# Last two projection units done slice by slice, with the first DeltaNet block prepared between the slices

## The reference

```python
h = rms_norm(x, g_mix)
proj = h @ w_in                       # q, k, v, z, b, a of DeltaNet; q, k, v and indexer of the sparse attention
y_a = gated_deltanet(...)             # chunks of 64 tokens, 4 heads:
#   gamma = exp(decay_i - decay_j) below the diagonal
#   A = strict_lower((k*beta) @ k.T * gamma);  T = inv(I + A)
#   u = T @ v*beta;  w = T @ k*beta*exp(decay);  qk = q @ k.T * gamma
#   scan over the 16 chunks:  v_new = u - w S;  o = q S + qk v_new;  S = S*last + k_dec.T v_new
y_b = indexed_sparse_attention(...)   # keep the 256 best keys of each query, softmax over these
x += concat(y_a, y_b) @ w_out;  x += cross_attention(...);  x += swiglu(...)
```

## Time and profile before

| what | us |
|---|---|
| median of 3 runs | 1855.81 |
| lowest, highest | 1853.48, 1856.25 |
| the profiled execution, its own time | 1854.56 |
| its span, first to last instruction | 1852.8 |
| PE busy | 1758.6 (95%) |
| DVE, ACT, POOL busy | 828.9, 675.0, 708.6 |
| mean granted TensorE clock | 0.974 of full |

### The profile page before, as it was taken

The page is one execution under the profiler, slowest core; times in us unless marked ns, Lnnn a source line. Parts: engine busy times, 40 slices in busy tenths (PEclk is TensorE's granted clock), DMA queues, the critical chain, the costliest instruction groups (busy, mean ns, idle before and its releaser), DMA issues.

```text
span 1852.8 us, 26846 instructions
## 1 busy us (share of the span) xinstructions
PE 1758.6 (95%) x10357; PEld 1410.4 (76%) x10357; DVE 828.9 (45%) x1436; ACT 675.0 (36%) x1414; POOL 708.6 (38%) x436
## 2 busy tenths in 40 slices
PE   6999999999987879799999999999999999999999
PEld 5888878877765665466877777888888888888887
DVE  4289878611115886565664365321331331233133
ACT  5366587688841223566035633010010001001000
POOL 4322234333232442464343225334424443343431
PEclk9999999999995999799999999999999999999999
DMA  7130111222230021002111011111111111111112
GB/s 235 55 83 24 35 35 46 69 91 80 80 126 1 2 93 50 21 2 92 62 31 46 24 35 34 50 54 46 45 45 57 45 45 57 45 45 45 57 34 91
DMA packets 112028, 102.33 MB, mean 55 GB/s; under 512 B 5132, under 2 KB 99391, under 8 KB 111679
## 3 DMA queue, kind: packets, MB, share of 16 engines
q1 hardware_dynamic: 109630, 92.67, 16.4%
q10 hardware_dynamic: 2304, 8.39, 1.1%
HBM read 87.42 MB, written 13.63 MB: 55 GB/s over the span
## 4 chain that ended last, share of the span: by engine, by line
PE 86%; DVE 7%; ACT 2%; issue 2%; SPq 1%; POOL 1%; DMA 0%; DVEq 0%; ACTq 0%
PE ps L1393 9%; PE ps L1395 9%; PE ps L1394 9%; PE ps L409 7%; PE ps L437 7%; PE ps L439 7%; PE ps L438 7%; PE ps L410 6%; PE ps L411 6%; PE ps L975 2%; PE ps L1224 2%; PE ps L1070 2%; PE ps L1249 2%; PE ps L1235 2%; PE ps L927 1%
## 5 line engine op out<-in xcount | busy, mean ns | idle before, releaser
L749 POOL TENSOR_TENSOR WS<-WR,zero 128x1024 fp32r<-128x1024 f32 (+1 forms) x119 | 228.2, 1918 | 883.5 <-PE ps L411 303.6
L751 POOL TENSOR_TENSOR WS<-WR,WS 128x1024 fp32r<-128x1024 f32 (+1 forms) x119 | 302.6, 2543 | 9.4
L1393 PE MATMUL ps<-HS,WS 128*128 128x512 f32 x704 | 274.7, 390 | 3.2 <-DVE HS L345 3.2
L1395 PE MATMUL ps<-HS,WS 128*128 128x512 f32 x704 | 274.4, 390 | 0.0
L1394 PE MATMUL ps<-HS,WS 128*128 128x512 f32 x704 | 274.1, 389 | 0.0
L456 DVE TENSOR_TENSOR X<-X,ps 128x512 f32<-128x512 f32 x272 | 183.8, 687 | 156.8 <-PE ps L439 155.3
L409 PE MATMUL ps<-HS,WS 128*128 128x512 f32 (+2 forms) x592 | 227.3, 384 | 3.8 <-ACT raw L1517 3.8
L410 PE MATMUL ps<-HS,WS 128*128 128x512 f32 (+2 forms) x592 | 224.5, 379 | 0.0
L411 PE MATMUL ps<-HS,WS 128*128 128x512 f32 (+2 forms) x592 | 224.2, 379 | 0.0
L2220 DVE TENSOR_TENSOR prod<-sil,ps 128x512 f32<-128x512 f32 x44 | 30.3, 688 | 394.7 <-PE ps L1395 394.7
L1740 ACT ACTIVATE sil<-ps 128x512 f32<-128x512 f32 x44 | 26.3, 598 | 395.0 <-PE ps L1395 395.0
(11 more groups left out here) (302 smaller groups left out, 2939.7 us busy)
## 6 DMA issues: line engine op xcount, KB each, us to landing
WR<-in_w_gu SPq DMA_DIRECT2D x44, 512.0 KB, 3.8
WR<-in_w_in SPq DMA_DIRECT2D x36, 512.0 KB, 3.8
WR<-in_w_down SPq DMA_DIRECT2D x22, 512.0 KB, 3.6
X<-in_x SPq DMA_DIRECT2D x8, 1024.0 KB, 8.4
dsa_spill<-cacc ACTq DMA_DIRECT2D x12, 512.0 KB, 2.6
KW<-in_w_xkv SPq DMA_DIRECT2D x8, 512.0 KB, 4.8
WR<-in_w_out SPq DMA_DIRECT2D x8, 512.0 KB, 3.6
out<-X SPq DMA_DIRECT2D x8, 512.0 KB, 2.6
```

The lines of the kernel that those rows point to most:

```text
L749: pool.tensor_tensor(hi, w, bc(zero1[:, 0:1], [P, cols]), ALU.add).then_inc(w_hi, 1)
L751: pool.tensor_tensor(lo, w, hi.bitcast(F32), ALU.subtract).then_inc(w_split, 1)
L1393: pe.matmul(ps[:, b0 + half, :], lo, HS[:, 0, k, c], start=(k == 0), stop=False)
L1395: mm = pe.matmul(ps[:, b0 + half, :], hi, HS[:, 0, k, c], start=False, stop=(k == KT - 1))
```

## The change

Units 14 and 15 (`LAST2`) leave the unit loop. They are done together by `last_two(k, first)`, one slice of the contraction for both, 12 matmuls a slice, into four banks (4 to 7) that keep accumulating, in the order 6, 5, 4, 3, 2, 1, 0, 7. `gdn_order` gets a step `beside`, which runs before each part of block 0: slices 6 and 5 stand before `diff`, slices 4, 3, 2 behind GQ, halves of slices 1 and 0 before z1, y2, z2, y3, and slice 7 before z3. The meeting and its waits are gone. A semaphore `hs_done` counts slices 6, 5, 4, 3 as done, and those who write over a slice wait for it (POOL at 1 for `gU` and at 4 for X0, DVE at 4 for A). ACT's copies and spills of the two units stand in part "k" of block 0. `PREP` has a new order for all blocks: k behind level 3, v behind level 4. A and Q move from part "k" to part "gq" on DVE, X0 to "gq" and TT0 before X1 on POOL, k and v go through banks 1 and 3, and z5 waits for `vb0`. The split of the second output weight (n = `N_OUT` + 1) moves on POOL behind X5 of block 0. `sd` on ACT moves from v = 13 to v = 12. The masks start later: the thresholds at p = 10 to 14 and not 2 to 8, the first mask at 15 and not 8, and from p = 28 on the table is the old one. SP loads `vraw` after the spills and `rsH`, `kD` behind the k transposes of block 3 and `zS` behind its v transposes.

```diff
+        PREP = (["gq", "x0"] + [f"{x}{s}" for s in (1, 2, 3) for x in "yz"]
+                + ["k", "y4", "z4", "v", "y5", "z5", "w", "next"])
+        LAST2 = (N_Z + 14, N_Z + 15)
...
+            run(beside, "diff")
             prep(-1, "next")
             for part in PREP:
+                run(beside, part)
                 prep(0, part)
...
-            sp.wait_ge(met, 3 * MEET_MIX)
+            d0d.wait(sp, "rs")
...
+            gp.wait(sp, "k1", 3)
+            sp.dma_start(kD[:, :, :], back[1]).then_inc(qk_in[1], 16)
             gp.wait(sp, "v1", 3)
-            sp.dma_start(kD[:, :, :], back[1]).then_inc(qk_in[1], 16)
...
-            for n in range(RING, N_OUT + RING - 1):
+            for n in range(RING, N_OUT + 1):
...
-                    pool.wait_ge(met, 3 * MEET_MIX)
                     g0d.wait(pool, "bk2")
+                    pool.wait_ge(hs_done, 1)
...
-                if part == "k":
+                if part == "gq":
                     gd.wait(pool, "A", b)
+                    if b == 0:
+                        pool.wait_ge(hs_done, 4)
...
+                    if b == 0 and part == "z3":
+                        split_of(N_OUT + 1)
...
-            for v in range(16):
+            for v in range(14):
                 up_pe(pe, N_Z + v, HS, WHOLE)
...
-            meet(0, pe)
+            def last_two(k, first, ready=None):
+                for i in first:
+                    n = LAST2[i]
+                    if k == 6:
+                        pe.wait_ge(w_split, n + 1)
+                    for half, (c, w) in enumerate(WHOLE):
+                        if ready:
+                            ready[i][half]()
+                        acc = ps[:, 4 + 2 * i + half, 0:w]
+                        hi, lo = (WS[:, n % RING, s, k * P:(k + 1) * P] for s in (0, 1))
+                        pe.matmul(acc, lo, HS[:, 0, k, c:c + w], start=(k == 6), stop=False)
+                        pe.matmul(acc, hi, HS[:, 1, k, c:c + w], start=False, stop=False)
+                        mm = pe.matmul(acc, hi, HS[:, 0, k, c:c + w], start=False, stop=(k == 7))
+                    if k == 7:
+                        mm.then_inc(unit_done, 1)
+                    elif i == 1 and k >= 3:
+                        mm.then_inc(hs_done, 1)
+            def beside(part):
+                if part == "diff":
+                    last_two(6, (0, 1), ...)
+                    last_two(5, (0, 1))
+                    pe.wait_ge(up_freed, ups[N_Z + 13] + 1)
+                elif part == "x0":
+                    for k in (4, 3, 2):
+                        last_two(k, (0, 1))
+                elif part == "z1":
+                    last_two(1, (0,))
...
+                elif part == "z3":
+                    last_two(7, (0, 1))
...
+                        if s == 5:
+                            gd.wait(pe, "vb0", b)
...
+            def beside(part):
+                if part == "k":
+                    spill(14)
+                    spill(15)
...
-            MASKS = {8: [(2, "count"), (2, "tie")], 10: [(2, 0), (2, 1)], 12: [(2, "kept"), (2, "out"), (2, "bias")],
+            MASKS = {15: [(2, "count"), (2, "tie")], 16: [(2, 0), (2, 1)], 17: [(2, "kept"), (2, "out")],
...
             def threshold(p):
-                if p == 2:
+                if p == 10:
+                    dve.wait_ge(unit_done, ups[LAST2[1]] + 1)
...
-                if part == "k":
+                if part == "gq":
...
+                    if b == 0:
+                        dve.wait_ge(hs_done, 4)
                     gd.mark(dve.tensor_tensor(Am[:, :], ps[:, 2, :], gam[:, 0, :], ALU.mult), "A", b)
```

More of the change, by code:

```diff
@@ L500, in build_layer @@
         g0d = steps("g0_dve", ["z", "max", "sp", "g", "ek", "rk2", "eq", "bk2", "ned", "ked"])
-        gp = steps("gdn_pe", ["diff", "GQ", "k0", "k1", "v0", "v1"]
-                   + [f"{x}{s}" for s in LV for x in "yz"] + ["w0", "w1"])
-        gd = steps("gdn_dve", ["A", "Q", "nk0", "kd0", "nk1", "kd1", "T0", "vb0", "vb1"]
-                   + [f"{x}{s}" for s in LV for x in (("T", "TT") if s < 5 else ("TT",))])
+        gp = steps("gdn_pe", ["diff", "GQ"] + [f"{x}{s}" for s in (1, 2, 3) for x in "yz"]
+                   + ["k0", "k1", "y4", "z4", "v0", "v1", "y5", "z5", "w0", "w1"])
+        gd = steps("gdn_dve", ["A", "Q", "T0"] + [f"{x}{s}" for s in (1, 2, 3) for x in ("T", "TT")]
+                   + ["nk0", "kd0", "nk1", "kd1", "T4", "TT4", "vb0", "vb1", "TT5"])
+        hs_done = sem("x_slices_done")
         ga = steps("gdn_act", ["gam"] + [f"y{s}" for s in LV] + ["w0", "w1"])
-        gl = steps("gdn_pool", ["gU", "dM", "gD", "X0", "X1", "TT0"] + [f"X{s}" for s in LV if s > 1])
+        gl = steps("gdn_pool", ["gU", "dM", "gD", "X0", "TT0", "X1"] + [f"X{s}" for s in LV if s > 1])
         sp_, sd_ = steps("scan_pe", ["v", "s", "o"]), steps("scan_dve", ["S", "ot"])
@@ L578, in bc @@
             return ap.to_broadcast(shape)
-        PREP = ["gq", "k", "x0", "v"] + [f"{x}{s}" for s in LV for x in "yz"] + ["w", "next"]
+        PREP = (["gq", "x0"] + [f"{x}{s}" for s in (1, 2, 3) for x in "yz"]
+                + ["k", "y4", "z4", "v", "y5", "z5", "w", "next"])
+        LAST2 = (N_Z + 14, N_Z + 15)
         def half_unit(e):
@@ L591, in bc_bank, with gdn_order @@
             return e % 3 if e < 8 else e % 2
-        def gdn_order(prep, tail, new_v=None, from_state=None, to_state=None, out=None):
+        def gdn_order(prep, tail, new_v=None, from_state=None, to_state=None, out=None, beside=None):
             def run(step, c):
@@ L837, in decayed @@
                 last = lastb[:, :].rearrange("p (a k) -> p a k", a=2)[:, :, 2 * (c + 1):2 * (c + 1) + 2]
+                if c == 0:
+                    for s in spilled:
+                        pool.wait_ge(s, 16 * 8)
                 sd_.wait(pool, "S", c)
@@ L1019, in _ @@
                     g0p.mark(mm, "cols")
-            meet(0, pe)
+            def last_two(k, first, ready=None):
[17 more added lines that the diff above has]
+                if part == "diff":
+                    last_two(6, (0, 1), ((lambda: g0a.wait(pe, "rows"), lambda: g0a.wait(pe, "last")),
+                                         (lambda: g0d.wait(pe, "eq"), lambda: d0a.wait(pe, "sd"))))
+                    last_two(5, (0, 1))
[5 more added lines that the diff above has]
+                    last_two(1, (0,))
+                elif part == "y2":
+                    last_two(1, (1,))
+                elif part == "z2":
+                    last_two(0, (0,))
+                elif part == "y3":
+                    last_two(0, (1,))
+                elif part == "z3":
+                    last_two(7, (0, 1))
             def per_unit(b, fn):
@@ L1209, in tail @@
                     o_tr(3 * (h - 5) // 2 + 2)
-            gdn_order(prep, tail, new_v, from_state, to_state, out)
+            gdn_order(prep, tail, new_v, from_state, to_state, out, beside)
             for t in range(T_ON, TT):
@@ L1533, in _, with spill @@
             act.wait_ge(silu_ev, 12)
-            for v in range(16):
+            def spill(v):
                 n = N_Z + v
@@ L1545, in _ @@
                 act.dma_start(z_dram[v] if v < 4 else d_dram[v - 4], cacc[:, v % 2, :]).then_inc(spilled[v % 2], 16)
+            for v in range(14):
+                spill(v)
                 if 2 <= v < 10:
@@ L1561, in _ @@
                     d0a.mark(act.activation(sqd[:, :], cacc[:, v % 2, :], ACT.Square), f"sq{D_UNITS[v - 4]}")
-                if v == 13:
-                    d0p.wait(act, "st3")
-                    d0a.mark(act.activation(sdH[:, :], ps[:, 7, :], ACT.Sqrt, bias=eps_t[:, 0:1], scale=1.0 / SD), "sd")
                 if v == 12:
@@ L1567, in _ @@
                     g0a.mark(act.activation(bk[:, :], ek[:, :], ACT.Sqrt), "bk")
+                    d0p.wait(act, "st3")
+                    d0a.mark(act.activation(sdH[:, :], ps[:, 7, :], ACT.Sqrt, bias=eps_t[:, 0:1], scale=1.0 / SD), "sd")
                 if v < Z_SLOTS:
@@ L1570, in _ @@
                         counts(h, rankA)
-            for s in spilled:
-                act.wait_ge(s, 16 * 8)
-            meet(1, act)
+            def beside(part):
+                if part == "k":
+                    spill(14)
+                    spill(15)
             def prep(b, part):
@@ L1638, in from_state @@
                     qa_.mark(ins, "qs", c - 1)
-            gdn_order(prep, tail, new_v=new_v, from_state=from_state)
+            gdn_order(prep, tail, new_v=new_v, from_state=from_state, beside=beside)
             squares(TT - 1)
@@ L1952, in _ @@
             d0d.mark(dve.reciprocal(rsH[:, :], sdH[:, :]), "rs")
-            meet(2, dve)
             def v4(t, c0=0):
```

46 lines of the change are left out of this document (23 added, 23 removed).

## The result

The changed kernel takes 1841.72 us in the median of four runs (1841.15 to 1842.54); the kernel before took 1855.18 us in the median of its four (1853.48 to 1856.25). The ratio is 0.9929, with an interval of 0.9911 to 0.9946. The forecast was 1838.5 with a range of 1830 to 1849. The profiled execution took 1842.54 us, 0.8 above the median; its span is 12.0 us shorter than before, where the sum said 17.1.

What follows compares the result with a forecast made beforehand. PE, busy 95% of the span, was taken as the bound, with gains where it idles or its clock is low (543 to 602 us). -23.2 + 2 + 4.1 = -17.1 from 1854.56 gave 1837.5; forecast 1838.5, range 1830 to 1849.

Steps and rivals of the forecast that it cites:

- The meeting and the overlap: Between unit 13 and the scan: PE's 5.1 us standstill goes, slices fill block 0's chain; scan starts 23.2 us earlier.
- The rival that the change does not do what it says: Block 0's chain is not filled, PE waits at a slice and levels run alone; 1841 us, chance 4%.
- The idle before y1 of block 0: PE waits 1.8 us for POOL's X0, TT0 and X1, y1 at 540.2; PE is full from there.
- z5, w and the clock there: End of block 0: z5 waits for `vb0`, then w and `diff` run at 1.2 GHz; +2 us (0 to +3.5).
- Blocks 2 and 3: Without the clock charge, block 2 even at 36.3 us, block 3 at 35.2 against 37.82 (-2.6); PE stands 4.3 us before y1.
- The charge of 1.5 us for the clock: Blocks 1 to 3, each: low clock behind 4.3 us of idle in the first step, between 0 and 1.7; +4.5 in all.
- Block 1: First block beside the scan: moved mask work makes DVE late, 40 us, +2 (0 to +6), before the clock charge.
- the rival of the masks: DVE bounds block 1 and into block 2: 6 us of moved work plus three 0.9 us collisions; 1845 us, chance 16%.
- The collision of DVE and POOL: Block 1: masks beside X0, TT0 and X1 exclude POOL's steps about once, 0.9 us, more than the +2; 1839.4.
- The clock rivals: Gaps cost no clock: 1832, 16%. Clock stays down through all three blocks: 1877, 3%; one block low: about 1851, 4%.
- one sign of being wrong: In the profile after: a block that had the clock at half for over 8 us.
- The other signs: Scan's first `v` 21 to 24 us earlier; idle 4 to 5.5 before y1; block 1 40 to 43, block 3 35 to 37.

Runs made afterwards that it cites:

- slices_first: Changed kernel with all eight slices of units 14 and 15 ahead of `diff`, none between the steps of block 0; 1850.5 us, ratio 0.9975.
- masks_after: Changed kernel with all of block 0's threshold work on DVE moved behind the subtraction of z5; 1837.2 us, ratio 0.9899.
- warm: Changed kernel with unused identity matmuls on PE before y1 in blocks 1 to 3 (34, 22, 22); 1841.6 us, ratio 0.9933.
- no_masks: Changed kernel without the mask steps of tiles 2 and 3 at p = 16 to 22; 1839.3 us, ratio 0.9917.
- early: Changed kernel with thresholds in DVE's idle of block 0's levels 1 to 3, masks spread anew, plus slice_ahead and pool_order; 1830.9 us, ratio 0.9865.
- slice_ahead: Changed kernel with unit 14's half of slice 1 moved from before z1 to before y1 of block 0; 1838.7 us, ratio 0.9914.
- pool_order: Changed kernel with TT0 and X1 right behind X0 on POOL, ahead of Sl; 1839.7 us, ratio 0.9916.

## Why the prediction was right, point by point

**The meeting and the overlap: right.** `diff` at 527.40 behind POOL's `gU` with 0.22 us of idle (forecast 527.2), X0, TT0 and X1 as counted, PE full from y1 to z3, ACT's spills and POOL's split without a wait for them. The rival that the change does not do what it says is out: slices_first shows what that would have looked like, and it costs 8.8 us. Its price in the prediction, 1841, was wrong by 9.5: slices_first took 1850.5, since levels 1 to 3 ran at 1.2 GHz there, where the sum of the rival had them at full clock.

**The idle before y1 of block 0: its length right, its price missed.** The sum had 1.8 us of idle there and charged nothing for it, since the only gap with a price was the one of 4.53 us. Measured: 2.10 us, then y1 at 1.54 and six slice matmuls at 0.43 in place of 0.23 each. Of the 3.0 us by which the end of z3 is late (558.4 for 555.3), 0.8 is y1's start, 0.4 y1 itself and 1.3 these six matmuls; the rest is about 0.15 us around each product between slices. This is the term of the sum that was mis-sized in the front; from z3 to the scan the forecast holds to 0.1 us (17.6, and 17.7 in the sum with its +2).

**z5, w and the clock there: right.** z5 behind 2.22 us for `vb0` (forecast 2.3), w at 3.68 and `diff` at 2.07, the +2 of the sum. masks_after confirms it by taking the cause away: waits of 0.70 and 0.79, w at 2.00.

**Blocks 2 and 3: right.** y1 behind 4.52 us with POOL's X1 as releaser (forecast 4.3), at 1.97; the blocks 0.5 and 0.3 us under the forecast. The idle of y2 in block 3 is gone. The charge of 1.5 us for the clock is about the 1.6 that warm gives for it.

**Block 1: mechanism right, size off.** The sum had +2 over before and 1.5 for the clock, 41.5; measured 44.6, between the sum and the rival of the masks (8.7 in place of 2). Measured against the steps of the sum (11.7, 8.4, 7.7 and 8.5, with 1.5 for the clock: 37.8) the block is 6.8 us over, of which the 41.5 had foreseen 3.7 without a place for them. Two places carry it. The first scan step took 16.1 us where I had 13.2. DVE and POOL in that step of the changed kernel:

```profile
580.76 0.68 DVE L2027 TENSOR_TENSOR blk<-ps,gam 128x512 f32<-128x512 f32 x1
581.36 1.37 DVE L1921 TENSOR_TENSOR_SCAN orderW<-ones,tieW 128x256 f32<-128x256 f32 x1
582.76 0.48 DVE L1921 TENSOR_TENSOR_SCAN orderW<-ones,orderW,tieW 128x128 f32<-128x128 f32 x1
583.28 0.69 DVE L2078 COPY S<-ps 128x512 f32<-128x512 f32 x1
```

```profile
580.92 1.26 POOL L821 TENSOR_TENSOR Xm<-Am,Lev 128x512 f32<-128x512 f32 x1 [2.88 <-DVE Am L2026]
584.15 1.04 POOL L851 TENSOR_TENSOR Sl<-S,lastb 128x512 f32<-128x512 f32 x1 [1.96 <-DVE S L2078]
585.14 1.26 POOL L824 TENSOR_TENSOR blk<-I,Xm 128x512 f32<-128x512 f32 x1
586.36 2.80 POOL L812 TENSOR_TENSOR gam<-Am,Lev 128x512 f32<-128x512 f32 x2
```

Two mask steps (line 1921) stand between Q and S on DVE. I had said that S is ready when Sl wants it, since DVE now does A, Q and S; I had not counted what `MASKS` puts between them. S is 1.85 us later for it, and POOL's Sl, TT0 and X1 all hang behind S. With GQ partly at half clock (0.9 more) and X1 slower (0.3) that is about the 2.9 us. no_masks, which leaves these steps out, shows it: S starts 0.60 us behind Q (578.46 and 577.86) and not 2.52, the idle before y1 is 5.06 us, and the first step takes 13.7. The last scan step took 12.9 us where I had 8.5, by four waits of PE for DVE:

```profile
608.94 0.66 PE L1170 MATMUL ps<-S,blk 128*64 128x128 f32 x8 [0.67 <-DVE S L2076]
610.42 1.15 PE L1118 MATMUL ps<-Tm,gam 64*64 64x64 f32 x32 [0.82 <-DVE Tm L2052]
...
613.50 1.15 PE L1118 MATMUL ps<-blk,Ym 64*64 64x64 f32 x32 [1.29 <-DVE blk L2045]
...
616.98 2.00 PE L1144 MATMUL ps<-blk,nkbd 64*128 64x64 f32 x32 [1.74 <-DVE blk L2057]
```

These add up to 4.5 us, while the two steps between took 0.6 less than forecast. early, with fewer mask steps there, has the last scan step at 8.5. DVE is busy 35.2 of 44.6 us (forecast 34.2), so the load was sized well. What was wrong is the step from load to time: I took a sum of busy time and a sum of waiting (34.2 and 6), but the waiting is met at the places where a mask stands right ahead of a result that PE or POOL wants.

**The collision of DVE and POOL: came true.** The scan of 256 elements took 1.37 us beside X0 and 0.69 without it (594.20 in the same trace). The Trainium skill, "SBUF — State Buffer", section "Who interferes with whom", has a DVE instruction with two SBUF inputs contend with a GpSimd one that reads SBUF; by that rule the trace agrees. The 0.9 us that the prediction had for one collision in block 1 is about the 0.7 of this scan and 0.3 of X1. But it was not the only collision in the block: behind it two mask steps of 384 elements took 0.97 and 1.50 us beside X1 and X2 (587.08 and 588.08), and 0.62 each in early, where POOL is idle beside them. What these cost in time no run shows.

**The clock rivals.** That the gaps cost no clock fell: y1 of each block took 1.97. That it stays down through a block fell too (block 1 at 0.85, the others 0.91). But one sign of being wrong that the prediction named did appear, a block at half clock for over 8 us: the row is the first step of block 1, and its 0.61 means some 12.6 us at half clock (an estimate: 0.39 of 16.1 us are missing, and half clock misses 0.5), about 5 of them idle. The sign took no account of idle, in which no product runs. The other signs held but for block 1: its idle before y1 (6.99 us for 4 to 5.5) and its length (44.6 for 40 to 43).

```profile
575.99:592.11 16.12, 9.13 (x154) 8.30 (x154) 8.75 (x13) 1.58 (x3) 9.12 (x7) 0.61 0.01 1
```

**Loads: right.** `kD` and `zS` are at nothing: from step 12 to the end the kernel takes 1146.6 us, and took 1146.7 before.

In sum: the front 3.0 and block 1 3.1 us too good, blocks 2 and 3 together 0.8 too bad, and the changed kernel's profiled execution 0.8 above its median where that of before was 0.6 below. That is why the medians differ by 13.5 and the spans by 12.0. It also means that some luck is in the forecast of the median: it missed by 3.2 us, the sum behind it by 5.2.

## What to carry to other kernels

A unit of matmuls that needs nothing can be cut up and laid into the waits of a chain of small products: this took 9 us of serial time here, and PE had 0.90 of full clock in it where the levels alone had half. But the work of another engine that stood in those waits has to go somewhere, and it costs where it stands right ahead of a result that is waited for, not by its sum; look for it by name between two instructions of that engine, in the order that the table of the schedule gives. And a new order that helps the lonely block need not be given to the blocks that have company: with the old one there, the side work in DVE's own idle, and the two small edits of slice_ahead and pool_order, the same idea won 35 us in place of 13.5.
